# One sum for two norms, gates as features, and attention heads woven with their output projection, in a two-block transformer kernel

## The chip, the cores and the metric

The kernel runs on one core of a Trainium2 chip. A core has TensorE (PE; matmuls, fed by weight loads, PEld), VectorE (DVE), ScalarE (ACT), GpSimd (POOL) and SyncE (SP), each with its own instruction stream; they meet by semaphores. The metric is the time of one execution in microseconds (us), lower is better, given as the median of several runs.

## The reference

256 tokens of width 1024 go through two different blocks, all in float32. The first is a gated short convolution, an FFN, latent attention and another FFN; the second a modulated block with a banded attention and an mLSTM branch, and a lookup among 16384 experts. What the change touches:

```python
# first block, layer 1 (latent attention), second half of it
q = (rms_norm(h @ w_dq, q_norm_g) @ w_uq).reshape(b, s, N_HEADS, 128 + 64)
q_pe = apply_rope(q[..., 128:], cos_h, sin_h)
p = softmax(where(mask, (q_nope @ k_nope.T + q_pe @ k_pe.T) * 192 ** -0.5, neg))
h = h + (p @ v).reshape(b, s, 8 * 128) @ w_o
h = h + (silu(hn @ w1) * (hn @ w3)) @ w2            # hn = rms_norm(h, mla_ffn_norm_g)
x = rms_norm(h, final_norm_g)
# second block
mod = silu(c) @ w_ada + b_ada                       # sh1, sc1, gt1, sh2, sc2, gt2
proj = (rms_norm(x, norm1_g) * (1 + sc1) + sh1) @ w_in
qkb = silu(causal_depthwise_conv(qkb, conv_w, conv_b))   # 4 taps, 1024 channels
y_a = chunk_band_attention(qa, ka, va, rel_bias)         # 8 heads of 64, with a bias
y_b = sigmoid(ob) * rmsnorm(mlstm_chunkwise(qb, kb, vb, ib, fb), mlstm_norm_g)
y = sigmoid(ga) * (y_a @ w_branch_a) + sigmoid(gb) * (y_b @ w_branch_b)
x = x + gt1 * (y @ w_out)
# then 8 heads of product-key lookup over 16384 experts, and a last rms_norm
```

## The kernel before

Weights come as one stream of 522 blocks of 128 x 1024 (512 KB), in the order of use, through a ring of three slots (`RING`). SyncE loads `raw`, ScalarE rounds it to a high part `wh` (helper `hi`, L932), VectorE takes the rest `wl` (helper `lo`, L1318); both run two blocks ahead (`ahead`, `LEAD`). The activations are split the same way (`xh`/`xl`, `yh`/`yl`, `hidh`/`hidl`, `lath`/`latl`), and TensorE forms each product of 128 x 128 with 256 tokens by three matmuls (helper `three`, L457 to L459): 24 in a block. Attention products, sums for the norms (`norm_sums`, L509) and the column sums of the modulation (`mod_sums`, L552) are single float32 matmuls.

PSUM is eight banks: `wk` (4; three of them for blocks in turn, the last for sums of squares) and `acc` (4; the FFN's output, or attention tiles). There is no scheduler: every engine's order is written out in its own function, and the same stage appears in each of them.

- *Latent attention* (`attention("latent")`): six query blocks `uq` are computed and read by VectorE, the last two are the halves for the rotation, which VectorE does behind the sixth (L1633 to L1640). Then for each of 8 heads: scores `scores(i + 1)` (L667 with 128 rows, L669 with 32 rows, for two query halves), `turn(i)` (transpose of the probabilities, L680), `mix(i - 1)` (L689, L690). VectorE masks and takes the maximum (L1657, L1660), ScalarE the exponent (L1115) and copies the transposed tile to `pt` (L1134), VectorE divides (L1666, L1667) and splits the mixed head into `yl` (L1687) after ScalarE's `yh` (L1122). VectorE also adds pieces of the modulation (`ada_piece`, L1454).
- *Output projection* (`add_out("attn_out", ...)`): 8 blocks by output features, each over all heads, with the next norm's sums two blocks behind.
- *FFN* (`ffn`): 22 steps of gate, up and down blocks. Its norm is applied late: the products start from the unscaled `h`, the root comes while they run.
- *Final norm, mixing norm*: `norm_sums("final")`, 32 column sums, then `norm_sums("mix")` on the scaled `h`; ScalarE takes the roots (L958), VectorE the reciprocal (L1335), the scaled chunks (L1338) and their low parts (L1352).
- *Projection*: `proj(0)` the 8 gate columns by tokens (48 matmuls with 8 columns), `proj(1)` to `proj(8)` the queries and keys of the mLSTM, whose convolution VectorE does per block: copy `u` (L1735), first tap (L1737), three more (L1741); `proj(9)` to `proj(16)` values by tokens, then the other features to `proj(44)`.
- *mLSTM units*: 8, each beside two projection blocks. Then `proj(29)`, the norm of the heads (`ms`, L1205, L1812), their transposes two banks in turn (L806), gating (L1820, `yh` L1209, `yl` L1823), and the band attention with two projection blocks in each head.

## Time and profile before

| | |
|---|---|
| median of 3 runs | 1773.52 us (1765.55 to 1783.88) |
| the profiled execution | 1779.25 us, its span 1777.6 |
| TensorE busy | 1681.3 us, 95% |
| VectorE busy | 1336.6 us, 75% |
| ScalarE busy | 856.6 us, 48% |
| mean granted clock of TensorE | 0.96 |
| chain that ended last | TensorE 78%, VectorE 15% |

The profile is of one execution. Busy time of an engine says nothing of how fast it runs: TensorE's clock has two levels, 1.2 and 2.4 GHz, and the granted clock is 0.5 or 1.0 of the higher one (a stretch with both lies between). An engine that is idle elsewhere costs nothing. So the views to read are busy time and clock by stretches, and the waits of TensorE.

### The profile page before, as it was taken

The numbers are of one execution on the slowest core, as the hardware profiler recorded it, in microseconds if no ns is written. First come the engines' busy times: TensorE is split into PE (matmuls) and PEld (weight loads), VectorE is DVE, ScalarE is ACT, GpSimd is POOL, SyncE is SP. The second block draws the span as 40 slices with busy tenths as digits, with TensorE's granted clock in tenths as the row PEclk, the third lists the DMA queues.
The fourth block names the chain that finished last, engine by engine and source line by source line (L and its number), as shares of the span: only waits on it lengthen the run. The fifth ranks groups of instructions, "written<-read, shape, count | busy, mean of one in ns | idle before, by whom it ended". The sixth has DMA issues, their size and how long they took to land.

```text
span 1777.6 us, 38130 instructions
## 1 busy us (share of the span) xinstructions
PE 1681.3 (95%) x13536; PEld 1632.9 (92%) x13536; DVE 1336.6 (75%) x2141; ACT 856.6 (48%) x1336; POOL 94.4 (5%) x180
## 2 busy tenths in 40 slices
PE   5999999889999998889979999999999999999997
PEld 5999999767999998788879999999999999999997
DVE  4767777876677756666655799997999788888886
ACT  4354444633444443456445554454555545445443
POOL 0000000000000000000000000000000021211210
PEclk8999999976999997999999999999999999999999
DMA  5547777433577643443335576775555577777773
GB/s 174 187 156 228 248 247 250 145 112 109 199 245 247 217 142 131 143 138 112 131 131 175 184 228 218 225 224 162 167 172 162 181 244 240 240 243 239 241 242 129
DMA packets 107467, 338.05 MB, mean 190 GB/s; under 512 B 13296, under 2 KB 29680, under 8 KB 107024
## 3 DMA queue, kind: packets, MB, share of 16 engines
q1 hardware_dynamic: 75600, 275.81, 48.1%
q0 software_dynamic: 13232, 44.19, 8.3%
q10 hardware_dynamic: 18576, 17.28, 2.8%
q8 instruction: 35, 0.57, 0.1%
q14 instruction: 24, 0.20, 0.0%
HBM read 319.79 MB, written 17.43 MB: 190 GB/s over the span
## 4 chain that ended last, share of the span: by engine, by line
PE 78%; DVE 15%; ACT 3%; issue 3%; DMA 1%; ACTq 0%; DVEq 0%; SPq 0%
PE wk L457 14%; PE wk L459 14%; PE wk L458 14%; PE acc L457 9%; PE acc L458 9%; PE acc L459 9%; DVE wl L1318 5%; PE acc L878 3%; PE wk L509 2%; PE wk L669 1%; ACT wh L932 1%; PE wk L667 1%; PE wk L552 1%; DVE idx L1846 1%; DVE uc L1741 1%
## 5 line engine op out<-in xcount | busy, mean ns | idle before, releaser
L932 ACT ACTIVATE wh<-raw 128x1024 fp32r<-128x1024 f32 x522 | 551.9, 1059 | 520.2 <-PE acc L459 237.5
L1318 DVE TENSOR_TENSOR wl<-raw,wh 128x1024 fp32r<-128x1024 f32 x522 | 638.3, 1225 | 196.4 <-ACT wh L932 193.7
L457 PE MATMUL wk<-xh,wh 128*128 128x256 f32 x2432 | 698.6, 287 | 39.9 <-DVE wl L1318 28.0
L459 PE MATMUL wk<-xh,wl 128*128 128x256 f32 x2432 | 684.0, 281 | 0.0
L458 PE MATMUL wk<-xl,wh 128*128 128x256 f32 x2432 | 683.9, 281 | 0.0
L457 PEld LDWEIGHTS wk<-xh,wh 128*128 128x128 f32 x2432 | 465.1, 191 | 48.0 <-DVE wl L1318 30.3
L459 PEld LDWEIGHTS wk<-xh,wl 128*128 128x128 f32 x2432 | 466.9, 192 | 0.0
L458 PEld LDWEIGHTS wk<-xl,wh 128*128 128x128 f32 x2432 | 464.9, 191 | 0.4
L457 PE MATMUL acc<-ph,wh 128*128 128x256 f32 x1024 | 282.7, 276 | 2.2 <-DVE pl L1966 2.2
L458 PE MATMUL acc<-pl,wh 128*128 128x256 f32 x1024 | 282.6, 276 | 0.0
L459 PE MATMUL acc<-ph,wl 128*128 128x256 f32 x1024 | 282.6, 276 | 0.0
L457 PEld LDWEIGHTS acc<-ph,wh 128*128 128x128 f32 x1024 | 192.2, 188 | 2.4 <-issue 2.4
L458 PEld LDWEIGHTS acc<-pl,wh 128*128 128x128 f32 x1024 | 192.2, 188 | 0.0
L459 PEld LDWEIGHTS acc<-ph,wl 128*128 128x128 f32 x1024 | 192.2, 188 | 0.0
L444 POOL DMA_DIRECT2D acts<-put_off x125 | 67.1, 537 | 1012.5 <-DVE w L1962 1008.7
L1962 DVE TENSOR_TENSOR w<-acts,gates 128x256 f32<-128x256 f32 x128 | 82.1, 642 | 29.6 <-DVE pl L1966 27.5
L1232 ACT ACTIVATE acts<-wk 128x256 f32<-128x256 f32 x128 | 49.3, 385 | 112.2 <-PE wk L459 112.2
L457 PE MATMUL acc<-hidh,wh 128*128 128x256 f32 x352 | 99.1, 281 | 2.3 <-DVE hidl L1502 2.3
L458 PE MATMUL acc<-hidl,wh 128*128 128x256 f32 x352 | 98.9, 281 | 0.0
L459 PE MATMUL acc<-hidh,wl 128*128 128x256 f32 x352 | 98.9, 281 | 0.0
L1924 DVE TENSOR_TENSOR hot<-cst,i_t 128x1024 f32<-128x1024 f32 x64 | 78.0, 1219 | 1.6 <-ACT i_t L1264 1.1
L457 PE MATMUL wk<-yh,wh 128*128 128x256 f32 x216 | 64.3, 298 | 10.1 <-DVE yl L1439 3.6
(271 smaller groups left out, 1951.3 us busy)
## 6 DMA issues: line engine op xcount, KB each, us to landing
raw<-stream SPq DMA_DIRECT2D x522, 512.0 KB, 4.2
ada_w<-ada POOLq DMA_DIRECT2D x48, 512.0 KB, 4.8
put_off<-acts ACTq DMA_DIRECT2D x125, 128.0 KB, 3.2
acts<-put_off POOLq DMA_DIRECT2D x125, 128.0 KB, 3.2
bias<-band_bias POOLq DMA_DIRECT2D x1, 1536.0 KB, 6.8
h<-x_in SPq DMA_DIRECT2D x2, 512.0 KB, 6.7
sk<-sub_keys POOLq DMA_DIRECT2D x1, 1024.0 KB, 8.2
out<-sq SPq DMA_DIRECT2D x1, 1024.0 KB, 3.9
```

The costliest lines, as they stand in the source:

```text
L444: pool.dma_start(acts[:, k], row).then_inc(act_back[k], 16)
L457: pe.matmul(out_ap, a_hi, b_hi, start=start, stop=False, skip_group_check=skip)
L458: pe.matmul(out_ap, a_hi, b_lo, start=False, stop=False, skip_group_check=skip)
L459: return pe.matmul(out_ap, a_lo, b_hi, start=False, stop=stop, skip_group_check=skip)
L509: mm = pe.matmul(norm_bank(name), const("ones"), sq[:, c], start=c == 0, stop=c == n - 1)
L552: mm = pe.matmul(wk[:, MOD_BANK, j:j + 1], ada_acc[:, part, (j % DC) * P:(j % DC + 1) * P], const("ones")[:, 0:1], start=True, stop=True)
L878: mm = pe.matmul(acc[:, 2 + par, j * P:(j + 1) * P], hot[:, par, 1, j], hot[:, par, 0, j], start=True, stop=True)
L932: nc.scalar.activation(wh[:, blk[0] % RING], raw[:, blk[0] % RING], ACT.Copy).then_inc(hi_ready, 1)
L1232: nc.scalar.activation(acts[:, k], wk[:, k, 0:T], ACT.Gelu_apprx_tanh).then_inc(act_ready, 1)
L1318: v.tensor_tensor(wl[:, s], raw[:, s], wh[:, s].bitcast(F32), ALU.subtract).then_inc(lo_ready, 1)
L1924: v.tensor_tensor(hot[:, par], const("iota").unsqueeze(1).unsqueeze(1).to_broadcast([P, 2, 4, P]), columns_of(slice(0, 2)).unsqueeze(3).to ...
L1962: v.tensor_tensor(w32[:], acts[:, k], g, ALU.mult).then_inc(w_ready, 1)
```

## The change

The order of the instructions is changed at three places, and the work a little.

*Latent attention.* The weights of the query blocks are sorted so that the rotated halves come first; blocks go to six different banks, ScalarE copies the last four, VectorE rotates out of banks 1 and 2 of `acc`. The output projection is cut by heads instead of by output features, and its block for head i - 2 follows the mix of head i - 1; it gathers in all four banks of `acc`, so the heads use `wk`. The FFN behind it starts with two blocks side by side, and its sums follow them. On TensorE, one head before (scores, turn, mix, next scores):

```order
L667 MATMUL wk<-kn,qn 128x128
L669 MATMUL wk<-kpe,qpe 128x128 x2
L667 MATMUL wk<-kn,qn 128x256
L669 MATMUL wk<-kpe,qpe 128x256 x2
L680 MATMUL acc<-cst,pr 128x128 x3
L689 MATMUL acc<-pt,vm 128x256
L690 MATMUL acc<-pt,vm 128x128
L667 MATMUL wk<-kn,qn 128x128
```

and after the change (the three rows of `three` stand eight times there, of which the first are shown):

```order
L670 MATMUL wk<-kn,qn 128x128
L672 MATMUL wk<-kpe,qpe 128x128 x2
L670 MATMUL wk<-kn,qn 128x256
L672 MATMUL wk<-kpe,qpe 128x256 x2
L685 MATMUL wk<-cst,pr 128x128 x3
L694 MATMUL wk<-pt,vm 128x256
L695 MATMUL wk<-pt,vm 128x128
L463 MATMUL acc<-yh,wh 128x256
L464 MATMUL acc<-yl,wh 128x256
L465 MATMUL acc<-yh,wl 128x256
```

Behind each mix now stand 24 matmuls of the output projection of an earlier head, before the next scores.

*Final and mixing norm.* With g the final gain, the mixing norm of the normed h is h g / sqrt(mean(h^2 (g^2 + eps)) + eps^2). So the squares are taken of `h` times `gs` = sqrt(g^2 + eps), and the first projection blocks need one sum and one root. The final norm's own sum comes later, behind the mLSTM units, and `h` is scaled in the heads of the band attention. The first two parts of the modulation are finished inside the second FFN. On TensorE behind the second FFN, before:

```order
L459 MATMUL acc<-hidh,wl 128x256
L509 MATMUL wk<-sq,cst 128x256 x8
L552 MATMUL wk<-cst,ada_acc 128x1 x32
L509 MATMUL wk<-sq,cst 128x256 x8
L457 MATMUL wk<-wh,xh 128x8
L458 MATMUL wk<-wl,xh 128x8
L459 MATMUL wk<-wh,xl 128x8
```

and after the change:

```order
L465 MATMUL acc<-hidh,wl 128x256
L515 MATMUL wk<-sq,cst 128x256 x8
L559 MATMUL acc<-cst,ada_acc 128x1 x32
L463 MATMUL wk<-xh,wh 128x256
L464 MATMUL wk<-xl,wh 128x256
L465 MATMUL wk<-xh,wl 128x256
```

The second set of sums is gone from here, and projection starts with feature blocks: `proj(0)` is 24 matmuls of 256 columns, its 8 rows are transposed later (`gate_turned`). In `proj(1)` to `proj(8)` ScalarE makes the copy `u` (now two buffers) and the first tap.

*Heads of the mLSTM.* They are transposed all at once into four banks, `proj(30)` follows, and the wait for the gated heads moves to the first turn of the band attention. On ScalarE, behind the last unit, before:

```order
L1202 ACTIVATE uc,ms<-hb 128x128
L1205 ACT_TABLE_LOAD
L1205 ACTIVATE ms<-ms,cols 128x8
L932 ACTIVATE wh<-raw 128x1024
L1169 ACT_TABLE_LOAD
L1169 ACTIVATE ga<-wk 128x256
L1171 ACTIVATE ga<-ga 128x256
L1209 ACTIVATE yh<-uc 128x256 x4
L1115 ACTIVATE pr,stat<-sc,stat 128x128
```

and after the change:

```order
L1298 ACTIVATE uc,ms<-hb 128x128
L1009 ACTIVATE sq<-h 128x256 x2
L989 ACTIVATE wh<-raw 128x1024
L1305 ACT_TABLE_LOAD
L1305 ACTIVATE ms<-ms,cols 128x8
L1044 ACTIVATE sd<-wk,cols 128x256
L1265 ACT_TABLE_LOAD
L1265 ACTIVATE ga<-wk 128x256
L1267 ACTIVATE ga<-ga 128x256
L989 ACTIVATE wh<-raw 128x1024
L1265 ACTIVATE ga<-wk 128x256
L1267 ACTIVATE ga<-ga 128x256
L1311 ACTIVATE yh<-uc 128x256 x4
```

`ms<-ms,cols` is the root for the heads, `sd` that of the final norm, `ga` the sigmoid of a block in two steps, `yh<-uc` the copies of the gated heads. Two squares and one `wh` come ahead of the root, and a second block's sigmoid ahead of the copies.

The diff, cut to what the prediction speaks of:

```diff
 NORMS = [("conv", DC, 1), ("ffn1", DC, 1), ("mla", DC, 2), ("kvlat", KC, 1), ("qlat", QC, 1), ("ffn2", DC, 1),
-         ("final", DC, 0), ("mix", DC, 1), ("peer", DC, 1), ("final2", DC, 0)]
+         ("mix", DC, 1), ("final", DC, 0), ("peer", DC, 1), ("final2", DC, 0)]
...
-                features(block_no(first), b0, xh, xl, normed_before(norm))
-                norm_sums(norm, DC - 2)
-                features(block_no(first + 1), (b0 + 1) % RING, xh, xl)
+                if norm == "ffn1":
+                    features(block_no(first), b0, xh, xl, normed_before(norm))
+                    norm_sums(norm, DC - 2)
+                    features(block_no(first + 1), (b0 + 1) % RING, xh, xl)
+                else:
+                    two_features(block_no(first), [b0, (b0 + 1) % RING], xh, xl, normed_before(norm))
...
+            uq_bank = [acc[:, 1], acc[:, 2], acc[:, 3], acc[:, 0], wk[:, 2], wk[:, 3]]
+            def uq(k):
...
+            def latent_scores(i):
+                pe.wait_ge(rotated, 1 + i // 4)
+                pe.wait_ge(uq_read, i // 2 + 1)
...
+            def out_of_head(i):
+                blk = block_no(FIRST["attn_out"] + i)
+                ready(blk)
+                pe.wait_ge(mixed_lo, i + 1)
+                stop = i == HEADS - 1
+                for o in range(DC):
+                    mm = three(acc_tile(o), piece(wh, blk, o * P, o * P + P), piece(wl, blk, o * P, o * P + P),
+                               yh[:, i], yl[:, i], i == 0 and o % 2 == 0, stop, skip=True)
+                    if stop and o in (1, 3, 5):
+                        mm.then_inc(out_pair, 1)
+                mm.then_inc(block_used, 1)
+            for k in range(4):
+                uq(k)
+            pe.wait_ge(more_const_in, 16)
+            latent_scores(0)
+            uq(4)
+            latent_scores(1)
+            uq(5)
+            latent_turn(0)
+            for i in range(1, HEADS + 2):
+                if i + 1 < HEADS:
+                    latent_scores(i + 1)
+                if i < HEADS:
+                    latent_turn(i)
+                if i - 1 < HEADS:
+                    latent_mix(i - 1)
+                if i >= 2:
+                    out_of_head(i - 2)
...
                 def turn(i):
-                    n = h0 + i
-                    wait(pe, pt_ready, n - 1)
+                    n = HEADS + i
+                    if i == 0:
+                        pe.wait_ge(m_gated, BH)
+                    pe.wait_ge(pt_ready, n - 1)
...
-            norm_sums("final")
+            norm_sums("mix")
             for part in range(2, 6):
                 mod_sums(part)
-            norm_sums("mix")
-            pe.wait_ge(mod_ready, 1)
-            base = normed_before("mix")
...
+            proj0 = block_no(FIRST["proj"])
+            two_features(proj0, [proj0[0] % RING, (proj0[0] + 1) % RING], xh, xl, normed_before("mix"))
+            proj(2)
+            pe.wait_ge(gate_kept, 1)
+            for b in range(TB):
+                mm = pe.transpose(acc[:, 0, b * P:(b + 1) * P], sv[:, b * P:(b + 1) * P], const("ident"))
+            mm.then_inc(gate_turned, 1)
...
+            norm_sums("final")
             proj(29)
             pe.wait_ge(m_normed, 1)
             for i in range(BH):
-                wait(pe, m_gated, i - 1)
                 for b in range(TB):
-                    mm = pe.transpose(acc[:, i % 2, b * P:(b + 1) * P], hb[:, b, i], const("ident"))
+                    mm = pe.transpose(acc[:, i, b * P:(b + 1) * P], hb[:, b, i], const("ident"))
                 mm.then_inc(m_turned, 1)
-            pe.wait_ge(m_gated, BH)
+            proj(30)
+            pe.wait_ge(rooted, NORM_NO["final"] + 1)
             def two_more(i, half):
-                if 30 + 2 * i + half < 45:
-                    proj(30 + 2 * i + half)
-            attention("band", two_more)
+                if 31 + 2 * i + half < 45:
+                    proj(31 + 2 * i + half)
+            band_attention(two_more)
...
+                if name == "mix":
+                    sc_e.wait_ge(gs_ready, 1)
+                    nc.scalar.activation(sq[:, c], src[:, c], ACT.Square, scale=gs[:, c:c + 1]).then_inc(squares, 1)
+                else:
+                    nc.scalar.activation(sq[:, c], src[:, c], ACT.Square).then_inc(squares, 1)
...
+            def proj(k, load=True):
                 blk = block_no(FIRST["proj"] + k)
-                ahead(blk)
+                if load:
+                    ahead(blk)
+                if k == 0:
+                    used(blk)
+                    nc.scalar.activation(sv[:], wk[:, blk[0] % RING, 0:T], ACT.Copy).then_inc(gate_kept, 1)
+                elif k < 9:
+                    c = k - 1
+                    w0 = GAIN["conv2_w"] + CK * c
+                    used(blk)
...
+                    nc.scalar.activation(u[:, k % 2, CK - 1:], wk[:, blk[0] % RING, 0:T], ACT.Copy).then_inc(conv_kept, 1)
+                    sc_e.wait_ge(conv_kept, k)
+                    nc.scalar.activation(uc[:, CK * (k % 2)], u[:, k % 2, 0:T], ACT.Identity, scale=gv[:, w0:w0 + 1],
+                                         bias=gain("conv2_b", c)).then_inc(tapped, 1)
                 if 2 <= k < 10:
                     sc_e.wait_ge(conv2, k - 1)
...
+                if unit >= 4:
+                    square("final", 2 * unit - 8, h)
+                    square("final", 2 * unit - 7, h)
+            ahead(block_no(FIRST["proj"] + 29))
             sc_e.wait_ge(m_sq, TB * BH)
             nc.scalar.activation(ms[:, 5], ms[:, 4], ACT.Sqrt, bias=cols[:, 0:1], scale=1.0 / BD).then_inc(m_root, 1)
-            proj(29)
+            late_root("final")
+            proj(29, load=False)
+            proj(30)
             for i in range(BH):
                 sc_e.wait_ge(m_gated, i + 1)
                 nc.scalar.activation(yh[:, 4 + i], uc[:, i % 2], ACT.Copy).then_inc(m_hi, 1)
-            attention("band", lambda i, half: proj(30 + 2 * i + half) if 30 + 2 * i + half < 45 else None)
+            band_attention(lambda i, half: proj(31 + 2 * i + half) if 31 + 2 * i + half < 45 else None)
...
+            uq_ahead(0)
+            uq_ahead(1)
+            used(block_no(FIRST["uq"] + 1))
+            rotate(0)
+            uq_ahead(2)
+            rotate(1)
+            uq_ahead(3)
+            latent_mask(0)
+            uq_ahead(4)
+            divide(0, 0)
+            latent_mask(1)
+            uq_ahead(5)
+            for i in range(HEADS + 2):
+                if 1 <= i < HEADS - 1:
+                    latent_mask(i + 1)
+                if i >= 2:
+                    ahead(block_no(FIRST["attn_out"] + i - 2))
+                if 2 <= i < HEADS:
+                    ada_piece(19 + i)
+                if i + 1 < HEADS:
+                    divide(i + 1, 0)
+                if 1 <= i <= HEADS:
+                    dve.wait_ge(mixed_hi, i)
+                    v.tensor_tensor(yl[:, i - 1], wk[:, 3, 0:T], yh[:, i - 1].bitcast(F32), ALU.subtract
+                                    ).then_inc(mixed_lo, 1)
...
+            def first_mod():
+                dve.wait_ge(mod_summed, 2)
+                biased(0, 2 * DC, wk[:, MOD_BANK])
+                scaled_gain(0, "norm1")
+                chain(v.tensor_tensor(modg[:, 0], modg[:, 0], gv[:, GAIN["final"]:GAIN["final"] + DC], ALU.mult))
+                v.engine_nop().then_inc(mod_ready, 1)
+            ffn("ffn2", "ffn2", 1, range(27, 6 * DC), beside=first_mod)
+            for k in range(2):
+                v.memset(u[:, k, 0:CK - 1], 0.0).then_inc(set_up, 1)
+            norm("mix", h, splits=[(columns(modg[:, 0]), xh, xl, 0, 0)])
...
+            biased(2 * DC, 6 * DC, acc[:, 3])
+            scaled_gain(1, "norm2")
             v.engine_nop().then_inc(mod_ready, 1)
-            chain(v.memset(u[:, 0:CK - 1], 0.0))
-            norm("mix", h, splits=[(columns(modg[:, 0]), xh, xl, 0, 0)])
             def proj(k):
...
+            dve.wait_ge(rooted, NORM_NO["final"] + 1)
+            wait(dve, scaled, scaled_before("final"))
+            chain(v.reciprocal(rs[:], sd[:]))
+            def beside_band(i, half):
+                if 31 + 2 * i + half < 45:
+                    proj(31 + 2 * i + half)
+                if half == 1:
+                    v.scalar_tensor_tensor(out=h[:, i], in0=h[:, i], scalar=gain("final", i), in1=rs[:], op0=ALU.mult,
+                                           op1=ALU.mult).then_inc(scaled, 1)
+            band_attention(beside_band)
```

## Rows read from the trace of the kernel before

**Rows 1.** The page, parts 1, 2 and 5: engines, granted clock, groups with mean ns.

```profile
PE 1681.3 (95%) x13536; PEld 1632.9 (92%) x13536; DVE 1336.6 (75%) x2141; ACT 856.6 (48%) x1336; POOL 94.4 (5%) x180
...
PEclk8999999976999997999999999999999999999999
...
L932 ACT ACTIVATE wh<-raw 128x1024 fp32r<-128x1024 f32 x522 | 551.9, 1059 | 520.2 <-PE acc L459 237.5
L1318 DVE TENSOR_TENSOR wl<-raw,wh 128x1024 fp32r<-128x1024 f32 x522 | 638.3, 1225 | 196.4 <-ACT wh L932 193.7
...
L1232 ACT ACTIVATE acts<-wk 128x256 f32<-128x256 f32 x128 | 49.3, 385 | 112.2 <-PE wk L459 112.2
```

**Rows 2.** Busy time by stretches: start:end, length, busy us (instructions) per engine, clock, DMA.

```profile
378.00:434.00 56.00, 54.87 (x152) 37.38 (x152) 29.78 (x80) 13.31 (x47) 3.70 (x7) 0.51 0.19 57
403.20:410.04 6.84, 6.84 (x21) 4.72 (x20) 3.82 (x11) 1.66 (x7) 0.53 (x1) 0.50 0.25 77
434.98:463.40 28.42, 28.41 (x233) 28.01 (x233) 20.90 (x28) 15.97 (x26) 1.63 (x4) 1.00 0.72 236
653.70:657.20 3.50, 3.50 (x18) 3.11 (x18) 1.42 (x5) 1.87 (x6) 0.00 (x0) 1.00 0.43 150
657.20:666.70 9.50, 9.50 (x66) 9.47 (x65) 5.01 (x9) 4.89 (x10) 0.00 (x0) 0.74 0.00 0
666.70:677.00 10.30, 6.26 (x17) 4.73 (x16) 3.83 (x9) 1.38 (x3) 1.58 (x3) 0.67 0.67 255
677.00:731.50 54.50, 49.32 (x289) 46.13 (x290) 39.21 (x75) 23.56 (x32) 0.00 (x0) 0.80 0.32 107
789.90:809.60 19.70, 12.56 (x68) 10.37 (x66) 11.91 (x29) 10.14 (x22) 0.00 (x0) 0.74 0.27 86
820.40:828.30 7.90, 7.90 (x61) 6.96 (x59) 4.75 (x11) 5.00 (x12) 0.00 (x0) 1.00 0.41 133
```

**Rows 3.** Waits of TensorE, whole program: who waited for whom, us, times, longest.

```profile
PE wk L457 <- DVE xl L1352: 8.3, 3, 4.1
...
PE wk L667 <- DVEq L1641: 5.1, 1, 5.1
PE wk L457 <- DVE u L1735: 4.2, 1, 4.2
...
PE acc L806 <- DVEq L1813: 3.5, 1, 3.5
...
PE acc L806 <- DVE uc L1820: 1.7, 2, 0.9
```

**Rows 4.** Timeline of TensorE, last query block: start us, length us, instruction.

```profile
371.29 0.28 PE L459 MATMUL wk<-lath,wl 128*128 128x256 f32 x1
...
373.41 0.28 PE L459 MATMUL wk<-lath,wl 128*128 128x256 f32 x1
```

**Rows 5.** Timeline of TensorE, a band head: scores, turn, mix.

```profile
823.48 0.92 PE L657 MATMUL wk<-ka,qa 64*128 64x128 f32 x4
824.33 0.55 PE L680 MATMUL acc<-cst,pr 128*128 128x128 f32 x3
...
827.54 0.86 PE L697 MATMUL acc<-pt,va 128*64 128x256 f32 x4
```

**Rows 6.** Timeline of VectorE, a norm's reciprocal and one block of the convolution.

```profile
657.93 1.75 DVE L1335 RECIPROCAL rs<-sd 128x256 f32<-128x256 f32 x1 [2.81 <-ACT sd L958]
...
696.21 0.42 DVE L1735 COPY u<-wk 128x256 f32<-128x256 f32 x1
...
697.12 1.53 DVE L1741 SCALAR_TENSOR_TENSOR uc<-u,gv,uc 128x256 f32<-128x256 f32 x3
...
699.69 0.42 DVE L1735 COPY u<-wk 128x256 f32<-128x256 f32 x1
```

**Rows 7.** Timeline of VectorE, two gated heads before the band attention.

```profile
797.54 0.48 DVE L1820 SCALAR_TENSOR_TENSOR uc<-acc,gv,ob 128x256 f32<-128x256 f32 x1
...
798.85 0.48 DVE L1820 SCALAR_TENSOR_TENSOR uc<-acc,gv,ob 128x256 f32<-128x256 f32 x1
```

413 lines of the change are left out of this document (216 added, 197 removed).

## Prediction, made before the changed kernel ran

> **What bounds the kernel now.** I read the page first. TensorE is busy in 1681.3 of 1777.6 us, so only what shortens TensorE's own sequence can shorten the run; the row of the granted clock shows where it ran at the lower level (1.2 GHz instead of 2.4) [rows 1]. Then I read busy time by stretches at the places the change touches, and the waits of TensorE alone, to see who holds it there. Four stretches matter. (1) The latent attention, 378 to 434 us: TensorE is 54.87 of 56 us busy, but at a granted clock of 0.51; one head takes 6.84 us, without a gap [rows 2]. (2) The output projection behind it, 28.4 us at full clock [rows 2]. (3) From the end of the second FFN to the end of the value blocks of the next projection (657.2 to 731.5 us): 9.50 us of column sums, 10.30 us in which only 6.26 us are busy, and 54.5 us at a granted clock of 0.80 [rows 2]. (4) 789.9 to 809.6 us, before the band attention: 12.56 of 19.7 us busy [rows 2]. The longest single waits in them are 5.1 us for the rotation, 4.1 us for the first normed chunk (inside the 8.3), 4.2 us for the convolution's input, 3.5 us for the normalised heads [rows 3].
>
> **A. Latent attention and output projection woven together.** The stretch is from the last query block (its last matmul starts at 373.41 us [rows 4]) to the second gate block of the FFN: 61.3 us to the first output block at 434.98, 28.4 us with it to 463.4 [rows 2], and one more FFN block and the column sums, 6.4. TensorE's work in it is the same before and after: 8 output blocks, 2 FFN blocks, 8 sums, 16 column sums, 8 heads. A dense matmul follows the other by (373.41 - 371.29) / 18 = 0.118 us [rows 4], so a block of 24 is 2.83 us: 8 give 22.6, 2 give 5.7; 8 sums take 3.5 (the 3.50 us stretch of sums in [rows 2]), the 16 column sums 3.6 (32 of the 64 records, at full clock, an estimate). That is 35.4 us. The heads cost 8 x 6.84 = 54.7, the wait for the rotation 5.1, another before the output blocks the 0.9 left over [rows 2, 3]: together 96.1 us, which is the stretch. After the change the rotation runs between the query blocks, since blocks 0 and 1 now hold the rotated halves, and the 5.1 us go: its 12 operations by VectorE, which filled them, lie beside four query blocks. The chain of a head (mask, exponent, divide, transpose, copy, mix, split) lies beside an output block of 2.83 us instead of beside the next head alone. What a head costs at full clock no row shows. Lower bound: half of 6.84, 3.42. Upper: by the band heads, whose scores of 384 columns take 824.33 - 823.48 = 0.85 us at full clock; a latent head has three such products, 2.55, a turn of 0.3 and a mix of 0.86 [rows 5], 3.7; with operand switches between the 32-row and 128-row products perhaps 4.1. I take 3.7, the nearest rows: 29.6. Nothing covers the chains of the first heads and of the last; I take 2.5 us. If all at full clock: 35.4 + 29.6 + 2.5 = 67.5. I add 3 us for one fall of the clock in the first heads, where no output block stands between: 70.5 against 96.1, **-25.6**.
>
> Does VectorE keep up? In a head it is busy 3.82 us with mask, divide, split and one piece of the modulation; it now adds one low part of a weight block (1.225 us a piece): 5.05 us in a period of 3.7 + 2.83 = 6.5 [rows 1, 2]. ScalarE has 1.66 + 1.059 = 2.7 [rows 1, 2]. Both fit, with some 1.5 us to spare. The eight sums for the next norm are no longer woven between output blocks but stand behind two FFN blocks; same count, same 3.5 us. The chunks of the residual come from VectorE two operations at a time, 0.8 us by the length of the taps [rows 6], against 0.71 us that six matmuls take; beneath 1 us, left out.
>
> The clock decides this term. The row shows a TensorE that is 98% busy and yet stays at 1.2 GHz for the whole attention [rows 2], after an idle wait of 5.1 us [rows 3]. The band attention, whose heads alternate with two dense blocks, has 1.00 [rows 2]. The new stage lies between the two: 2.83 dense of 6.5 us. By the Trainium skill, "TensorE: Matmul & The Clock Gate", section "What's actually happening", the throttle is the default and activity releases it; by that rule a stage without idle time would be at the full level, and the term would be the -25.6; by the row of the latent attention alone the same stage would stay at 1.2 GHz, and the term would be positive (last rival). The trace does not agree with the rule taken simply: busy was not enough.
>
> **B. One sum and one root; gates as features; ScalarE copies the convolution's input.** The mixing norm is taken straight from the residual (squares scaled by the root of g^2 + eps), so in the stretch the scaling of the residual, the second root and 8 sums go, and the 32 column sums now lie between the sum and the first projection block. Before: 9.50 + 10.30 + 54.50 = 74.3 us. After: the column sums remain, 9.50 (the clock falls in them as before: 0.74 [rows 2]). The reciprocal of 1.75 us and 8 chunks of two operations, 0.8 us a chunk [rows 6], begin at the end of the sums; they end at about the time the column sums end, so the 4.1 us wait goes. Then nine blocks of features, the gates now among them (48 short matmuls become 24 of 256 columns): 9 x 2.83 = 25.5; two transposes 0.4; four value blocks of 12 matmuls at twice 0.118: 11.3. The first two blocks start at the low clock: by the 0.74 it held for 2 x 0.26 x 9.5 = 5 us of the column sums, and I let it hold for as long behind them: +2.4. The convolution: before, VectorE needs 699.69 - 696.21 = 3.48 us per block (copy, first tap, three taps, low part) [rows 6], more than 2.83, so it fell behind and TensorE waited 4.2 us. Without the copy and the first tap (0.91 us, 696.21 to 697.12) it needs 2.6, under 2.83, and ScalarE takes 1.06 and three passes of 0.385, 2.2 [rows 1]. TensorE sets the pace; left of the wait 0.9. Sum: 9.5 + 25.5 + 0.4 + 11.3 + 2.4 + 0.9 = 50.0, **-24.3**. Bounds: -27 with no low clock; -14 if the convolution still sets the pace at 3.5 us a block and the clock stays at 0.80. Left at nothing: the gate operands, asked for by GpSimd at the end of the column sums as before; VectorE now needs them only at block 3, some 12 us later.
>
> **C. Before the band attention.** The final norm's 8 sums move here: +3.5 us on TensorE, its 8 squares lie on ScalarE in the last four units (0.385 us each [rows 1]), its scaling in the band heads. All 8 transposes of the heads go at once, and block 30 follows, so the waits between them (3.5 + 1.7 [rows 3]) are partly filled. But ScalarE now stands at block 30's sigmoid before it copies the gated heads, and VectorE waits for these copies: (estimates from here on, from the order and these lengths) transposes done at about 799.3 us, block 30 at 802.2, its two ScalarE steps 0.8, then four gatings at 798.85 - 797.54 = 1.31 us [rows 7] until 808, a reciprocal of 1.75 [rows 6], the first masks 1.3, exponent and divide 1.2: the first turn at 812.3, against 809.6, where the stretch ends [rows 2]. TensorE has only the scores and block 31 to do meanwhile, and the second scores need the masks: a gap of about 5 us. By then it has done one block more (2.83). Against 809.6 that is 2.7 later with 2.8 more done, so level; with 0.9 us at the last head, which now has no block beside it, and 0.6 for the clock: **+1.5**. Bounds -4 (the copies come early) and +6 (the clock falls in the gap).
>
> **Sum.** -25.6 - 24.3 + 1.5 = -48.4. The profiled execution took 1779.25 us (span 1777.6, 1.65 around it): 1730.9. The median of the runs shown is 1773.5, 5.7 lower, so the forecast for a median is 1725.
>
> **Rivals.**
> - *The clock swings in the woven attention.* For: the low-row products of a head, at a stretch of 3.7 us, are the same that stayed at 1.2 GHz. Against: an output block and the mix stand between. Price: in each head some 5 us of its work at half speed, +2.6 x 8 = 21: 1746. The same title of the Trainium skill, section "A second HAM failure mode: psum-queue depth-cycling", describes such swinging from small idle times between matmul groups.
> - *The chain sets the pace.* VectorE has 5.05 us of work in order, with waits for ScalarE in the middle; if a head takes the band's 7.9 us instead of 6.5 [rows 2], +11: 1736.
> - *B gives half*, at its bound of -14: 1735.
> - *The low clock holds the whole stage* (slower). It fell in a pause and came back only with dense blocks. If it stays until the FFN: heads 54.7, output blocks 45.3, FFN blocks 11.3, sums and column sums 10.6, waits 2.5, together 124.4 against 96.1: +28. With B still at -19, because its clock stays at 0.80, and C at +6, +15: 1788. It decides if a granted clock under 0.6 shows between the first output block and the last. Against it: everywhere else dense blocks bring the clock back.
>
> **How the numbers follow.** Forecast 0.58, swinging clock 0.19, chain 0.12, B at half 0.06, low clock throughout 0.05. Range: low end with A -31, B -27, C -4, 1711; high end 1752, beyond the swinging clock with C at its bound. One per cent, 18 us, is about what a measurement tells from no change. Faster by more: the first four cases less their overlap, 0.93; same 0.05 (most of the slower case, and two of the weaker ones together), slower 0.02.
>
> **What would show it.** A: granted clock near 1 between the query blocks and the FFN, heads 6.2 to 6.9 us apart, 90 us shrunk to about 65 to 68. B: no wait for the first normed chunk, blocks 2.83 us apart, no wait of 4 us for the convolution. C: TensorE idle about 5 us before the second band scores, held by VectorE's gating, which waits for ScalarE. Wrong would be: a clock near 0.5 in A, or heads over 7.5 us; a wait for weights in B.

## The result, and the profile after

| | before | changed |
|---|---|---|
| median, same chip | 1769.53 us (1763.49 to 1783.88, 4 runs) | 1719.74 us (1714.93 to 1724.48, 4 runs) |
| the profiled execution, its span | 1779.25, 1777.6 | 1714.93, 1713.1 |
| TensorE busy; mean granted clock | 1681.3; 0.96 | 1629.2; 0.982 |

The changed kernel takes 0.9707 of the time before, 95% interval 0.9639 to 0.9775. It was forecast at 1725.

The page of the changed kernel, parts 1, 2 and 5, against [rows 1]. Its line numbers are larger: L463 to L465 are the former L457 to L459, L670 and L672 the scores, L685 the turn, L989 and L1420 the two parts of a weight block, L1334 the former L1232.

```profile
PE 1629.2 (95%) x13514; PEld 1592.6 (93%) x13514; DVE 1324.7 (77%) x2127; ACT 862.6 (50%) x1357; POOL 94.4 (6%) x180
...
PEclk9999999999999989999999999999999999999999
...
L1334 ACT ACTIVATE acts<-wk 128x256 f32<-128x256 f32 x128 | 49.0, 383 | 103.3 <-PE wk L465 103.2
```

The dip of the clock in slices 9 and 10 of [rows 1], at 7 and 6 tenths, is gone. Next, busy time by stretches of the changed kernel (columns as in [rows 2]): the latent attention with the output projection, up to the last column sum (A); one turn of its loop; the next FFN's two first blocks; from the first column sum to the end of the value blocks (B); from the last mLSTM unit to the branches (C); the entry to the band attention.

```profile
342.36:433.69 91.33, 88.03 (x597) 77.56 (x596) 68.14 (x137) 46.32 (x97) 3.16 (x6) 0.98 0.44 143
385.75:392.35 6.60, 6.60 (x46) 5.51 (x45) 4.84 (x12) 2.69 (x7) 0.53 (x1) 1.00 0.48 159
433.69:442.35 8.66, 8.66 (x51) 8.66 (x51) 4.59 (x7) 2.52 (x4) 0.00 (x0) 0.63 0.35 122
616.10:664.60 48.50, 47.94 (x331) 45.81 (x330) 35.85 (x65) 32.08 (x52) 1.58 (x3) 0.89 0.51 174
723.31:801.71 78.40, 70.90 (x500) 62.42 (x500) 51.34 (x113) 49.18 (x108) 0.00 (x0) 0.96 0.38 120
722.90:746.40 23.50, 16.77 (x111) 14.42 (x109) 14.20 (x31) 13.34 (x29) 0.00 (x0) 0.95 0.27 90
```

The same stretches A, B and C of the kernel before:

```profile
351.75:469.80 118.05, 111.28 (x598) 91.77 (x596) 81.03 (x150) 46.25 (x94) 5.81 (x11) 0.77 0.42 135
657.15:731.45 74.30, 65.08 (x370) 60.35 (x369) 48.05 (x92) 29.82 (x45) 1.58 (x3) 0.77 0.33 114
789.66:866.26 76.60, 68.35 (x487) 59.59 (x485) 46.74 (x103) 47.79 (x105) 0.00 (x0) 0.93 0.39 124
```

and its two first FFN blocks, which the sum below needs:

```profile
469.80:477.16 7.36, 7.36 (x51) 7.36 (x51) 2.00 (x4) 1.37 (x2) 0.00 (x0) 0.77 0.31 116
```

In A the number of matmuls is the same, 598 and 597, but they take 88.03 us instead of 111.28: what went is mostly time of TensorE's own work, at a clock of 0.98 in place of 0.77. In B 39 matmuls went (370 to 331), the idle time fell from 9.2 to 0.6 us, and the clock rose from 0.77 to 0.89. C kept its idle time, 8.25 and 7.50, and got 13 matmuls more. So A is 26.7 shorter, B 25.8, C 1.8 longer. Two smaller stretches between them: the FFN's first two blocks take 8.66 instead of 7.36 (from 469.80 to 477.16), since the low clock there lasts 6.4 us instead of 3.4 (other traces with the same code there take 5.85 to 8.66, by how long the clock is low), and the mLSTM units 58.7 instead of 58.2. Sum -26.7 + 1.3 - 25.8 + 0.5 + 1.8 = **-48.9**. The medians differ by 49.8, the two spans by 64.5; where the other 15.6 came from is the last section's.

Waits of TensorE in the changed kernel, whole program, against [rows 3]:

```profile
PE wk L735 <- DVE stat L1756: 4.8, 1, 4.8
...
PE wk L685 <- DVE pr L1764: 1.9, 1, 1.9
PE acc L863 <- DVEq L1948: 1.8, 1, 1.8
```

The 5.1 us for the rotation, one of the 4.1 for the first normed chunk and the 4.2 for the convolution are gone. New are 4.8 us before the second band scores and 1.9 at the last latent turn. ScalarE before the band attention (start, length, instruction, in brackets the idle time before it and who ended it):

```profile
736.21 0.38 ACT L1265 ACTIVATE ga<-wk 128x256 f32<-128x256 f32 x1 [3.43 <-PE wk L465]
736.62 0.42 ACT L1267 ACTIVATE ga<-ga 128x256 f32<-128x256 f32 x1
736.95 0.40 ACT L1311 ACTIVATE yh<-uc 128x256 fp32r<-128x256 f32 x1
```

and VectorE after it:

```profile
737.38 0.43 DVE L1958 TENSOR_TENSOR yl<-uc,yh 128x256 fp32r<-128x256 f32 x1 [2.94 <-ACT yh L1311]
...
741.63 1.75 DVE L1961 RECIPROCAL rs<-sd 128x256 f32<-128x256 f32 x1
743.41 0.29 DVE L1753 SCALAR_TENSOR_TENSOR sc<-wk,bias 128x128 f32<-128x128 f32 x1
```

ScalarE stands 3.43 us at block 30's sigmoid (`ga`), which waits for TensorE; the copy `yh` is queued behind it, VectorE waits 2.94 us for that copy, and the reciprocal of the final norm stands ahead of the first masks, for which TensorE waits 4.8.

### The profile page after: what moved, and what is told of

It is laid out like the page before. It is cut to its first block, busy times and chain, and to the rows that moved or that the text cites. A ratio compares the mean times of both kernels' runs of the same rounds, so it can differ in the third digit from the quotient of the medians.

```text
span 1713.1 us, 38109 instructions
## 1 busy us (share of the span) xinstructions
PE 1629.2 (95%) x13514; PEld 1592.6 (93%) x13514; DVE 1324.7 (77%) x2127; ACT 862.6 (50%) x1357; POOL 94.4 (6%) x180
## 4 chain that ended last, share of the span: by engine, by line
PE 82%; DVE 11%; ACT 3%; issue 2%; DMA 1%; ACTq 0%; DVEq 0%; SPq 0%
PE wk L463 15%; PE wk L464 15%; PE wk L465 15%; PE acc L463 10%; PE acc L464 10%; PE acc L465 9%; PE acc L935 3%; DVE wl L1420 3%; ACT wh L989 1%; PE wk L515 1%; PE wk L672 1%; PE acc L559 1%; DVE eq L2050 1%; DVE key L2052 1%; DVE eq L2048 1%
## 5 line engine op out<-in xcount | busy, mean ns | idle before, releaser
L989 ACT ACTIVATE wh<-raw 128x1024 fp32r<-128x1024 f32 x522 | 551.9, 1059 | 495.9 <-PE acc L465 239.6
L1420 DVE TENSOR_TENSOR wl<-raw,wh 128x1024 fp32r<-128x1024 f32 x522 | 637.9, 1224 | 204.2 <-ACT wh L989 201.6
L463 PE MATMUL wk<-xh,wh 128*128 128x256 f32 x2440 | 697.4, 286 | 40.0 <-DVE wl L1420 27.0
L465 PE MATMUL wk<-xh,wl 128*128 128x256 f32 x2440 | 682.6, 280 | 0.0
L463 PEld LDWEIGHTS wk<-xh,wh 128*128 128x128 f32 x2440 | 466.7, 191 | 47.3 <-DVE wl L1420 30.2
L465 PEld LDWEIGHTS wk<-xh,wl 128*128 128x128 f32 x2440 | 465.4, 191 | 0.0
L463 PE MATMUL acc<-ph,wh 128*128 128x256 f32 x1024 | 282.7, 276 | 2.2 <-DVE pl L2114 2.2
L465 PE MATMUL acc<-ph,wl 128*128 128x256 f32 x1024 | 282.6, 276 | 0.0
L463 PEld LDWEIGHTS acc<-ph,wh 128*128 128x128 f32 x1024 | 192.2, 188 | 2.4 <-issue 2.4
L465 PEld LDWEIGHTS acc<-ph,wl 128*128 128x128 f32 x1024 | 192.2, 188 | 0.0
L1334 ACT ACTIVATE acts<-wk 128x256 f32<-128x256 f32 x128 | 49.0, 383 | 103.3 <-PE wk L465 103.2
L463 PE MATMUL acc<-hidh,wh 128*128 128x256 f32 x352 | 97.4, 277 | 2.6 <-DVE hidl L1605 2.6
L465 PE MATMUL acc<-hidh,wl 128*128 128x256 f32 x352 | 97.2, 276 | 0.0
L935 PE MATMUL acc<-hot 128*128 128x128 f32 x512 | 66.9, 280 | 3.2 <-DVE hot L2076 3.2
```

Of the source, the lines that this page charges most:

```text
L463: pe.matmul(out_ap, a_hi, b_hi, start=start, stop=False, skip_group_check=skip)
L465: return pe.matmul(out_ap, a_lo, b_hi, start=False, stop=stop, skip_group_check=skip)
L935: mm = pe.matmul(acc[:, 2 + par, j * P:(j + 1) * P], hot[:, par, 1, j], hot[:, par, 0, j], start=True, stop=True)
L989: nc.scalar.activation(wh[:, blk[0] % RING], raw[:, blk[0] % RING], ACT.Copy).then_inc(hi_ready, 1)
L1334: nc.scalar.activation(acts[:, k], wk[:, k, 0:T], ACT.Gelu_apprx_tanh).then_inc(act_ready, 1)
L1420: v.tensor_tensor(wl[:, s], raw[:, s], wh[:, s].bitcast(F32), ALU.subtract).then_inc(lo_ready, 1)
```

## Experiments

The edits are to the changed kernel. Stretches are named as above; A, B and C are read from the same first to the same last matmul in each trace, and each figure for a stretch is that of one execution. Traces whose code for a stretch is that of the changed kernel show how far such a figure can be trusted: A is 90.3 to 91.3 us in six of them, B 48.5 to 49.4 in eight, C 77.5 to 79.1 in eight. The runs were made on several chips; the kernel before took 1771.14 us (median of 7) beside `e1_apart` to `e4_copies_first`, and 1786.50 (one run) beside `e5_sums_spread`, `e6_two_roots`, `e9_late_woven` and `e10_late_apart`.

### What keeps the clock up: dense blocks, or no pause?

**Theory 1:** TensorE stayed at 1.2 GHz in the attention before because a head's narrow products (most have fewer rows or columns than those of a dense block) don't bring the clock up; the output blocks between them now do. **Theory 2:** the clock fell in the wait for the rotation, and removing that wait was enough.

`e1_apart`: the output blocks stand behind all heads again; the early rotation stays.

```diff
-            for i in range(1, HEADS + 2):
+            for i in range(1, HEADS + 1):
...
-                if i >= 2:
-                    out_of_head(i - 2)
+            for i in range(HEADS):
+                out_of_head(i)
```

> The changed kernel with the eight output blocks taken out from between the heads and put behind the last head; the early rotation, the banks and the order inside the heads stay. Theory 1 (dense blocks between the heads hold the clock): the granted clock falls in the heads and stays near 0.5, a head takes about 6.8 us as before the change, the stretch from the first query block to the FFN grows from 83 to about 105 us or more, and the median is 20 to 28 us over 1719.7. Theory 2 (the idle wait for the rotation made the clock fall before, and without it the clock stays): granted clock near 1, and a head takes what the chain over ScalarE and VectorE takes, 4 to 5 us; the stretch grows by 4 to 11 us at most.

Measured: median 1728.99 (1722.99 to 1742.8, 4 runs), 0.9726 of before (0.9672 to 0.978). A takes 92.57 us. Stretches of it: A, and four heads in a row.

```profile
349.69:442.26 92.57, 88.91 (x597) 78.14 (x596) 68.19 (x137) 46.59 (x97) 3.16 (x6) 0.96 0.44 141
379.90:394.70 14.80, 14.80 (x80) 10.74 (x79) 13.33 (x40) 6.61 (x26) 1.58 (x3) 1.00 0.31 83
```

TensorE in it, the scores of one head and of the next:

```profile
379.97 0.39 PE L670 MATMUL wk<-kn,qn 128*128 128x128 f32 x2
...
383.65 0.39 PE L670 MATMUL wk<-kn,qn 128*128 128x128 f32 x2
```

Heads with nothing between them run at a clock of 1.00, 383.65 - 379.97 = 3.68 us each. The same products took 6.84 in [rows 2]. Theory 1 falls as stated: once up, the clock stays up through them. Only at the last head did it fall, for 6.8 us, at the end of a wait of 1.5 us; a wait of 1.0 us lies inside the low stretch. Theory 2's own figures were too high: it expected 4 to 5 us a head and a stretch longer by 4 to 11 us, and the stretch grew by 1.3.

`e10_late_apart` puts the wait back: six query blocks first, the rotation behind them, heads and output blocks apart. `e9_late_woven` has the same wait, with the blocks woven in. Their common edit (ScalarE's and VectorE's orders follow it):

```diff
-            for k in range(4):
+            for k in range(6):
                 uq(k)
             pe.wait_ge(more_const_in, 16)
+            pe.wait_ge(rotated, 2)
             latent_scores(0)
-            uq(4)
             latent_scores(1)
-            uq(5)
```

> The kernel with the output blocks apart (e1_apart), and the rotation put back behind the sixth query block, where TensorE waits for it as before the change. Heads and output blocks stand as in the kernel before; banks and weights as after. Theory 2, now mine after e1_apart (the idle wait drops the clock, and a head's products alone do not bring it back): granted clock near 0.5 over the heads, 6.8 us a head, the stretch from the first scores to the column sums of the FFN 90 to 94 us (76.0 in e1_apart, 91.0 in the kernel before). Rival (banks, or ScalarE's copies, made the difference): clock near 1 and about 76 us.

> The changed kernel, woven as it is, with the same late rotation: TensorE idles for about 4 to 5 us before the first scores. Theory: the clock falls in the wait, and the first dense output blocks bring it back; so it is low for 10 to 17 us only, and the stretch from the first scores to the column sums is 78 to 84 us. Then the weaving is worth 8 to 14 us wherever the clock has fallen, and nothing where it has not. Rival (a woven stage stays low too): over 100 us at a clock near 0.5.

Measured, one run each: 1762.71 and 1751.56 us. `e10_late_apart`, A and the heads:

```profile
343.61:465.21 121.60, 112.73 (x598) 93.15 (x596) 69.56 (x137) 47.08 (x97) 3.17 (x6) 0.75 0.33 107
370.60:430.30 59.70, 58.14 (x164) 40.31 (x165) 28.54 (x79) 14.64 (x49) 3.17 (x6) 0.50 0.17 53
381.25:388.09 6.84, 6.84 (x21) 4.73 (x20) 2.72 (x10) 2.40 (x9) 0.00 (x0) 0.50 0.00 0
```

`e9_late_woven`, A, the first stretch of the attention, the one behind it:

```profile
342.65:451.18 108.53, 99.06 (x597) 84.20 (x596) 68.62 (x137) 46.46 (x97) 3.17 (x6) 0.86 0.37 121
369.90:397.30 27.40, 27.40 (x89) 19.29 (x90) 10.40 (x31) 6.70 (x22) 0.00 (x0) 0.54 0.00 1
397.30:424.00 26.70, 26.14 (x174) 21.72 (x173) 18.68 (x45) 10.54 (x28) 2.11 (x4) 1.00 0.49 159
```

and the wait that both have in their lists, here from `e9_late_woven`:

```profile
PE wk L670 <- DVEq L1743: 6.1, 1, 6.1
```

Inside this wait of `e10_late_apart`, from 364.46 to 370.53, with no matmul in either stretch:

```profile
364.50:368.00 3.50, 0.00 (x0) 0.00 (x0) 3.19 (x7) 0.72 (x2) 0.00 (x0) 1.00 0.74 232
369.00:370.50 1.50, 0.00 (x0) 0.00 (x0) 1.34 (x4) 0.00 (x0) 0.00 (x0) 0.73 0.18 74
```

The granted clock is 1.00 in the first part of the wait and falls in the last 1.5 us of it, before any head has begun. The kernel before shows the same at the end of its 5.1 us (373.69 to 378.82), again with no matmul in the row; its clock fell at 378.48:

```profile
377.50:378.70 1.20, 0.00 (x0) 0.00 (x0) 1.03 (x3) 0.00 (x0) 0.00 (x0) 0.91 0.01 3
```

Together with the changed kernel these are the four corners of stretch A:

| A, us | heads alone | blocks woven in |
|---|---|---|
| TensorE waits 6.1 for the rotation | 121.6 | 108.5 |
| no such wait | 92.6 | 91.3 |

The wait costs 29.0 us where heads stand alone: 6.1 itself, and some 23 by the low clock that follows. Woven blocks bring the clock back, after 27 us of low clock and not the 10 to 17 that were expected, and are then worth 13.1. Without the wait they are worth 1.3 against this trace, 1.3 to 2.3 against the six traces of kernels whose code for A is the same (90.3 to 91.3). From the first scores to the last column sum, as the expectations count, it is 94.7 and 81.3 with the wait, 76.0 and 74.5 without. So both theories hold a part: the wait dropped the clock, the products of the heads did not bring it back (59.70 us at 0.50, TensorE busy for 58.14; which of their properties is to blame, the rows, the columns or the type, no run shows), and the weaving only repairs what the early rotation had already prevented. The corner of 121.6 is not the kernel before itself, whose A is 118.1: there the wait is 1.0 shorter and the clock low for 54.6 us instead of 61.4.

`e2_pairs`: output blocks two by two, behind every second head, to vary the density of the weaving.

```diff
-                if i >= 2:
-                    out_of_head(i - 2)
+                if i >= 3 and i % 2 == 1:
+                    out_of_head(i - 3)
+                    out_of_head(i - 2)
```

> The changed kernel with two output blocks behind every second head, so two heads (7.2 us of float32 products) stand between dense stretches of 5.7 us, instead of one and 2.8. Theory 1 (the clock needs dense blocks among any few heads): some falls of the clock in the heads, each 3.4 us or longer, and the stretch grows from 83 to 87 to 95 us. Theory 2 (only idle time counts): no fall but the one of the changed kernel; heads without a block behind them wait for their chain by 0.5 to 1.5 us, so the stretch grows by 2 to 6 us.

Measured: 1734.65 us, A 103.66, 12.3 more. It tested something else. VectorE, in its unchanged order, is at the low part of a block whose slot is still held by the block before it, so TensorE waits for the divided probabilities; the wait list over these heads:

```profile
PE wk L685 <- DVE pr L1765: 9.0, 3, 4.7
```

The clock fell 1.2 us behind the first wait (2.1 us long, to 383.82) and 1.1 behind the second (2.1, to 400.98), and inside the third (4.7, from 413.46), at 415.74. On density it says nothing, and it adds three cases of a fall with a wait.

### The convolution's input, and where the column sums lie

`e3_conv_vector`: VectorE copies `u` and makes the first tap again.

```diff
-                    nc.scalar.activation(u[:, k % 2, CK - 1:], wk[:, blk[0] % RING, 0:T], ACT.Copy).then_inc(conv_kept, 1)
-                    sc_e.wait_ge(conv_kept, k)
-                    nc.scalar.activation(uc[:, CK * (k % 2)], u[:, k % 2, 0:T], ACT.Identity, scale=gv[:, w0:w0 + 1],
...
+                    v.tensor_copy(u[:, k % 2, CK - 1:], wk[:, blk[0] % RING, 0:T]).then_inc(conv_kept, 1)
...
+                    chain(v.tensor_scalar(last, u[:, k % 2, 0:T], gv[:, w0:w0 + 1], gain("conv2_b", c), ALU.mult, ALU.add))
```

> The changed kernel with the copy of the convolution's input and the first tap back on VectorE. My account: VectorE then needs 3.5 us per block against 2.83 of TensorE, falls behind by about 0.65 us in each of eight blocks less what the buffers hold, and the first value block waits some 4 to 5 us again: the stretch from the column sums to the end of the value blocks grows from 48.7 to 53 us. Rival (this part is worth nothing, the low clock was what made the stretch long): the stretch stays within 1 us of 48.7.

Measured: 1730.29 us, B 57.50. B of it:

```profile
622.87:680.37 57.50, 50.97 (x331) 47.60 (x330) 42.61 (x81) 25.06 (x36) 1.57 (x3) 0.88 0.42 147
```

and its longest wait there:

```profile
PE wk L463 <- DVE u L1860: 4.2, 1, 4.2
```

The 4.2 us of [rows 3] are back to the tenth. But B is 9.0 longer, about twice what was expected: the long wait replaces one of 0.6, five small waits for low parts add 2.3, and the clock falls for 3.4 us just behind the long wait, so the value blocks take 12.7 instead of 11.1. That is 7.5; the rest lies in the column sums (9.6 instead of 9.1, where the clock fell earlier) and in a slower pace of the matmuls (last section), and need not be of the edit. Against the eight traces B is 8.1 to 9.0 longer, so what was removed had cost about twice its longest wait.

`e6_two_roots`: the final norm before the mixing norm again, on the column sums' other side, and the mixing norm from the scaled residual.

```diff
-         ("mix", DC, 1), ("final", DC, 0), ("peer", DC, 1)
+         ("final", DC, 0), ("mix", DC, 1), ("peer", DC, 1)
...
-            norm_sums("mix")
+            norm_sums("final")
             for part in range(2, 6):
                 mod_sums(part)
+            norm_sums("mix")
```

> The changed kernel with the final norm and the mixing norm one after the other again (sums, root, scaling of the residual, 32 column sums, second sums, second root); gates as features and ScalarE's copies stay. My account: the second sums, the wait for root and first chunk and the lower clock behind them return, so the stretch from the column sums to the end of the value blocks grows from 48.5 by 11 to 16 us, and the stretch before the band attention shrinks by 2 to 3.5 us since its 8 sums go. Rival (the scheme only moves the wait): it grows by under 6 us.

Measured: 1734.38 us, B 59.20, C 78.3. B of it, then two of its waits:

```profile
623.05:682.25 59.20, 54.61 (x347) 50.86 (x346) 41.01 (x74) 37.10 (x62) 1.58 (x3) 0.86 0.42 142
```

```profile
PE acc L863 <- DVEq L1940: 4.3, 1, 4.3
PE wk L463 <- DVE xl L1446: 4.0, 1, 4.0
```

One sum and one root for both norms is worth 10.7 us in B (9.8 to 10.7 against the eight traces), just under the low end of what was expected: 4.0 of wait for the first normed chunk and 6.7 of sums, which ran at the low clock. With the 9.0 of `e3_conv_vector` that is 19.7 of the 25.8 that the change gained in B; the largest piece left is the gates, whose 48 short matmuls took 10.2 us before (677.04 to 687.28, at the low clock) and are now one of the feature blocks. No run puts them back alone. C was expected 2 to 3.5 shorter without its 8 sums, and is not: the wait for the scaled heads (L863) grows from 1.8 to 4.3. The moved sums had been filling 2.5 us of that wait. The longer wait also dropped the clock (747.42 to 754.25), as the wait of 1.8 us in the changed kernel did not, while the wait before the second band scores is 3.1 instead of 4.8. All together, C without the 8 sums lies inside the 77.5 to 79.1 of the traces that have them: their 3.5 us cost nothing here that can be seen.

`e5_sums_spread`: the column sums stand between feature blocks 3 to 6, to keep the clock up.

```diff
             norm_sums("mix")
-            for part in range(2, 6):
-                mod_sums(part)
...
             for k in range(3, 13):
+                if k < 7:
+                    mod_sums(k - 1)
                 proj(k)
```

> The changed kernel with the 32 column sums taken from behind the mixing norm's sum and spread, 8 each, before projection blocks 3 to 6. My account: the column sums hide the root, the reciprocal and the first chunk, so TensorE now waits 4 to 5 us for the first chunk; in return the sums run at full clock (7.3 us in place of 9.2). The stretch from the end of the norm's sum to the first mLSTM product, 48.5 in the changed kernel, becomes 49 to 53 us. Rival (the low clock in the column sums costs more than the cover gives): 44 to 47 us, and it is a better version.

Measured: 1717.18 us. From the norm's first sum to the end of B it takes 53.96, the changed kernel 51.95 (612.65 to 664.60); without the 3.5 us of the sum itself, as the expectation counts, 50.5 against 48.5, inside the 49 to 53 expected. The stretch of this kernel:

```profile
610.40:664.36 53.96, 49.20 (x348) 46.00 (x347) 36.91 (x71) 34.41 (x59) 1.58 (x3) 0.97 0.46 165
```

The clock is 0.97 instead of 0.90, as hoped, but TensorE is idle for 4.8 us: nothing lies between the sums and the first block, and the wait of 4.0 for the first normed chunk is back. It shows that the column sums are the cover of that wait. They are better slow there than fast elsewhere, by 1 to 2 us in these traces.

### The order before the band attention

`e4_copies_first`: ScalarE copies the gated heads ahead of block 30's sigmoid.

```diff
             proj(29, load=False)
-            proj(30)
+            ahead(block_no(FIRST["proj"] + 30))
             for i in range(BH):
                 sc_e.wait_ge(m_gated, i + 1)
                 nc.scalar.activation(yh[:, 4 + i], uc[:, i % 2], ACT.Copy).then_inc(m_hi, 1)
+            proj(30, load=False)
```

> The changed kernel with one thing moved on ScalarE: the four copies of the gated heads come before block 30's sigmoid instead of behind it. My account of the wait before the second band scores (4.8 us): it is the chain that begins with these copies; the gating then starts 2.9 us earlier, the wait becomes about 1.9 us, the clock does not fall there (in the changed kernel it fell for 6.8 us), and the stretch from the last unit to the first branch block shrinks from 78.4 to 72 to 75 us. Rival (the wait belongs to the reciprocal and the masks): it shrinks by less than 1 us.

Measured: 1710.44 us, C 73.50. The wait before the second band scores:

```profile
PE wk L735 <- DVE stat L1757: 0.9, 1, 0.9
```

and C:

```profile
723.97:797.47 73.50, 69.76 (x500) 61.45 (x500) 51.18 (x113) 48.85 (x108) 0.00 (x0) 0.98 0.39 129
```

The wait fell from 4.8 to 0.9 and C by 4.9 us with an exchange of two steps in one queue. The cause read from the trace, ScalarE at the sigmoid, is shown. The clock does not fall behind this wait any more; the 0.98 comes from 3.4 us (733.53 to 736.95) behind the wait of 1.9 us for the normalised heads, where it did not fall in the changed kernel.

`e8_best` adds to this the final norm's reciprocal behind the first band softmax, and the last latent head's divide ahead of a low part. `e7_after_again` is the changed kernel itself on the same chip.

```diff
+                if i == HEADS - 2:
+                    divide(i + 1, 0)
                 if i >= 2:
                     ahead(block_no(FIRST["attn_out"] + i - 2))
...
-                if i + 1 < HEADS:
+                if i + 1 < HEADS and i != HEADS - 2:
                     divide(i + 1, 0)
...
-            chain(v.reciprocal(rs[:], sd[:]))
...
+                if i == 0 and half == 1:
+                    chain(v.reciprocal(rs[:], sd[:]))
```

> The changed kernel with three orders changed: the gated heads' copies before block 30's sigmoid (e4_copies_first), the reciprocal of the final norm behind the first softmax of the band attention, and the last latent head's divide ahead of the low part and the modulation piece on VectorE. Expected: the stretch before the band attention 72 to 73.5 us instead of 78.4, the wait of 1.9 us at the last latent turn gone and with it the fall of the clock at 408 us; the median 6 to 9 us below that of the changed kernel on the same chip. Rival (each freed wait is taken by the next one): under 3 us.

> The changed kernel once more, as the measure for e8_best and for the FFN's pace. Steps of the second FFN were 8.48 us in the kernel before and 8.16 in the changed one, with the same code. If the pace belongs to the program, it is 8.16 again in both FFNs; if it varies from execution to execution, either figure may show, and the kernel's times spread by about 7 us for each FFN.

Measured, beside a kernel before of 1780.27 us: `e8_best` 1714.12 (1706.65 to 1725.1, 6 runs), 0.9641 of before (0.9602 to 0.9681); `e7_after_again` 1724.88 (1711.94 to 1746.07, 6 runs), 0.9666 (0.9621 to 0.9712). A and C of `e8_best`:

```profile
343.38:431.79 88.41, 85.63 (x598) 75.56 (x596) 68.11 (x137) 46.22 (x97) 3.17 (x6) 1.00 0.45 148
725.44:797.34 71.90, 68.40 (x500) 59.92 (x500) 51.00 (x113) 48.85 (x108) 0.00 (x0) 1.00 0.40 132
```

By stretches it gains 90.86 - 88.41 = 2.5 us in A and 77.8 - 71.9 = 5.9 in C over `e7_after_again`, 8.4 together. The medians are 10.8 apart, but that rests on the two longest runs of `e7_after_again` (1737.83 and 1746.07); without them its median is 1718.98, 4.9 above `e8_best`, and the two intervals overlap. The times alone show no difference clear of their spread; the stretches carry the claim, one execution each. In C the clock no longer falls. Almost nothing of this is due to the reciprocal: C is 1.6 shorter than in `e4_copies_first`, and 1.5 of it lies before the first band scores, which come 12.8 us into C instead of 14.3 because the clock did not fall there this time. In A the rival came true in part: the wait of 1.9 at the last latent turn is gone, and the next one, for the mixed head's low part (`yl`), grew from 0.7 to 1.5.

## Why the prediction was right, and where it was not

**A: size right, cause half right.** Forecast -25.6, measured -26.7. The terms came out one by one: a head at full clock 3.7, measured 3.68; a turn of the loop 6.5, measured 6.60; VectorE in it 5.05, measured 4.84; one clock fall in the stretch, at the last head instead of the first ones. What failed is the reading of the row of 0.51. The text took the choice between 0.5 and 1.0 as one of density, the new stage lying between two examples. The corners of A show another cause: a wait for the rotation drops the clock, the heads do not bring it back, and the change took the wait away. The order of the query blocks alone, `e1_apart` against `e10_late_apart`, is worth 29.0; the weaving, on top of it, 1.3. The prediction had both facts side by side ("98% busy and yet stays at 1.2 GHz", "after an idle wait of 5.1 us") and priced the removed wait at 5.1 alone. That the size came out is partly luck: where a wait stands before woven heads (`e9_late_woven`), A is 17.2 longer than without it, and a sum that lets the blocks hold the clock would have allowed little more than the 6.1 of the wait.

**The rivals on the clock** got 0.24 for this reason. The swinging one did not come: one low stretch in A, of 3.4 us, behind the wait of 1.9, and in four of the six traces of this code none. By the Trainium skill, "TensorE: Matmul & The Clock Gate", section "A second HAM failure mode: psum-queue depth-cycling", small idle times between groups can make the clock swing; four heads in a row at 1.00, with no idle time, are no case of that rule. The nearest to it is `e2_pairs`, three falls with waits of 2.1, 2.1 and 4.7 us; a swing from idle times below 1 us no run here shows. The rival in which the low clock holds throughout needed a fall at the start, and no wait was left there to give it. Even with the wait it would not have held: in `e9_late_woven` the clock was back while blocks were still being woven in.

By the same title of the Trainium skill, section "What's actually happening", throttling is the default and activity releases it. With `e10_late_apart` the trace disagrees again: 58.14 us busy of 59.70 at a clock of 0.50.

**The chain as the pace** did not come: 6.60 a turn, TensorE busy for all of it. The 1.5 us of room that the text gave VectorE were there (4.84 in 6.60), except at the last head, where the divide stands behind a low part.

**B: right.** Forecast 50.0 for 74.3, measured 48.5 (48.5 to 49.4 in the eight traces). The wait for the first normed chunk went because the column sums cover it (`e5_sums_spread` brings it back), the convolution's went but for 0.6 (`e3_conv_vector` brings it back). Piece by piece: column sums 9.1 against 9.5, nine feature blocks with transposes and their low clock 27.8 against 28.3, wait 0.6 against 0.9, value blocks 11.1 against 11.3. About 1 us of the 1.5 is luck: the blocks ran at 0.113 us a matmul instead of 0.118 in this execution (last section). What the text gave no reason for is that the clock would stay up behind the first two blocks. It took them at full clock, rightly, because the two waits that it removed each had a fall with them (low for 17.1 us from 675.44, which lies in the wait before the first block, and for 6.8 from 716.40, in the convolution's); the convolution's 4.2 were worth 9.0.

**C: right, with its mechanism.** Forecast +1.5, measured +1.8; TensorE idle 4.8 us before the second band scores, forecast about 5, held by VectorE behind ScalarE at block 30's sigmoid. `e4_copies_first` removes it. The +3.5 for the moved sums was too much for a place with a wait in it (`e6_two_roots`). The clock's fall was priced too low: it lasted 6.8 us, 5.8 of them behind the gap, which at half speed is a loss of 2.9 against 0.6 allowed. The two errors cancel, so the mechanism of the gap is shown and the size is partly luck.

**The sum** was -48.4 and came out as -48.9, with two terms that it did not have (+1.3 in the FFN's first blocks, +0.5 in the units), whose errors cancel those of A, B and C (-1.1, -1.5, +0.3). For the profiled execution the forecast of 1730.9 was 16 too high (1714.93); most of that is the pace of the last section, which the prediction did not know.

## What to carry to other kernels

Where a stretch runs at the low clock, look first at what TensorE did just before it: a wait of 6.1 us cost 29 us here, because the products behind it did not bring the clock back, and a reorder of six blocks removes it. Price a removed wait with the low stretch behind it, two to five times its length in the cases measured here (8.1 to 9.0 us for 4.2, 17.2 and 29.0 for 6.1); and price a moved piece of TensorE's work by the wait that it fills at its new place and uncovers at the old one. Before a chain that TensorE waits for, read every engine's queue for one step that waits for TensorE and stands ahead of the chain.
